# Seven block products in place of eight in a feed-forward up-projection, with ScalarE and VectorE preparing their operands

## The reference

```python
def swiglu(h, w_up, w_down):
    gate, val = jnp.split(h @ w_up, 2, axis=-1)
    return (jax.nn.silu(gate) * val) @ w_down
...
        h = rmsnorm(x, norm_ffn[l]) * (1.0 + sc_ffn) + sh_ffn
        x = x + gt_ffn * swiglu(h, w_ffn_up[l], w_ffn_down[l])
    return rmsnorm(x, norm_final)
```

## Time and profile before

| | us |
|---|---|
| median of 3 runs (lowest, highest) | 2607.14 (2605.65, 2610.41) |
| the profiled execution | 2607.23 |
| its span | 2605.5 |
| TensorE busy (matmuls) | 2543.5, 98% of the span |
| VectorE busy | 1892.0, 73% |
| ScalarE busy | 997.7, 38% |
| GpSimd busy | 504.9, 19% |

### The profile page before, as it was taken

How to read it: one execution, slowest core, us unless ns; L and a number is a source line. 1 busy time by engine, 2 the same in 40 slices (tenths; PEclk the granted TensorE clock), 3 DMA queues, 4 the chain that set the end, 5 groups by cost and what they waited for, 6 DMA issues and landing times.

```text
span 2605.5 us, 44201 instructions
## 1 busy us (share of the span) xinstructions
PE 2543.5 (98%) x16256; PEld 2260.3 (87%) x16256; DVE 1892.0 (73%) x3606; ACT 997.7 (38%) x2220; POOL 504.9 (19%) x440
## 2 busy tenths in 40 slices
PE   6999999999999999999999999999999999999998
PEld 4899889889899989989989989989888888888887
DVE  5688778878878877777777777885666666666666
ACT  6643744654474373364355345333400000000002
POOL 1000401311220130000000000000344444433330
PEclk9999999999999999999999999999999999999999
DMA  7221231132122122223123213241121111111111
GB/s 238 61 65 30 58 80 38 36 94 50 33 70 62 26 57 80 43 50 86 42 48 87 46 33 97 71 135 51 50 65 49 49 45 46 48 49 49 49 41 65
DMA packets 221703, 160.85 MB, mean 62 GB/s; under 512 B 24720, under 2 KB 204024, under 8 KB 221488
## 3 DMA queue, kind: packets, MB, share of 16 engines
q1 hardware_dynamic: 208592, 149.98, 19.8%
q0 software_dynamic: 12896, 8.05, 3.1%
HBM read 141.67 MB, written 16.33 MB: 61 GB/s over the span
## 4 chain that ended last, share of the span: by engine, by line
PE 78%; DVE 14%; ACT 6%; issue 1%; DMA 1%; SPq 0%; DVEq 0%; ACTq 0%
PE bank L180 31%; PE bank L172 21%; PE bank L2191 9%; PE bank L1256 2%; PE bank L1009 2%; PE bank L1262 2%; DVE sig L1089 2%; PE bank L1590 1%; PE bank L1605 1%; PE bank L1213 1%; PE bank L1608 1%; PE bank L1606 1%; DVE feat_region L1702 1%; PE bank L1756 1%; DVE rows_region L1098 1%
## 5 line engine op out<-in xcount | busy, mean ns | idle before, releaser
L172 PE MATMUL bank<-wA_hi,h_hi 128*128 128x256 f32 x1024 | 296.5, 290 | 1.0 <-ACT sig L1061 0.4
L172 PE MATMUL bank<-wB_hi,h_hi 128*128 128x256 f32 x1024 | 296.4, 289 | 0.5 <-ACT sig L1061 0.2
L172 PE MATMUL bank<-wB_lo,h_hi 128*128 128x256 f32 x1024 | 295.5, 289 | 0.0
L172 PE MATMUL bank<-wA_lo,h_hi 128*128 128x256 f32 x1024 | 295.2, 288 | 0.0
L172 PE MATMUL bank<-wB_hi,h_lo 128*128 128x256 f32 x1024 | 295.0, 288 | 0.0
L172 PE MATMUL bank<-wA_hi,h_lo 128*128 128x256 f32 x1024 | 295.0, 288 | 0.0
L180 PE MATMUL bank<-h_hi,wA_hi 128*128 128x512 f32 x672 | 266.0, 396 | 3.1 <-DVE feat_region L1022 1.9
L180 PE MATMUL bank<-h_hi,wB_lo 128*128 128x512 f32 x672 | 265.7, 395 | 0.0
L180 PE MATMUL bank<-h_hi,wA_lo 128*128 128x512 f32 x672 | 265.7, 395 | 0.0
L180 PE MATMUL bank<-h_hi,wB_hi 128*128 128x512 f32 x672 | 265.7, 395 | 0.0
L180 PE MATMUL bank<-h_lo,wA_hi 128*128 128x512 f32 x672 | 265.4, 395 | 0.0
(11 more groups left out here) (394 smaller groups left out, 6042.8 us busy)
## 6 DMA issues: line engine op xcount, KB each, us to landing
w_raw<-in_w_in_dram SPq DMA_DIRECT2D x96, 512.0 KB, 4.0
w_raw<-in_w_ffn_up_dram SPq DMA_DIRECT2D x44, 512.0 KB, 3.9
rows_region<-in_ada_w_dram SPq DMA_DIRECT2D x64, 256.0 KB, 2.8
w_raw<-in_w_ffn_down_dram SPq DMA_DIRECT2D x22, 512.0 KB, 3.5
ada<-in_ada_w_dram SPq DMA_DIRECT2D x8, 1024.0 KB, 14.5
conv_in<-row_scratch SPq DMA_DIRECT2D x16, 512.0 KB, 4.5
rows_region<-in_x_dram SPq DMA_DIRECT2D x8, 512.0 KB, 6.8
w_raw<-in_w_in_dram SPq DMA_DIRECT2D x16, 256.0 KB, 2.9
```

The costliest lines, as they stand in the source:

```text
L172: mm = nc.tensor.matmul(bank[:, n_out:n_out + n1 - n0], (h_hi, h_lo)[hp][:, k, t * P:t * P + P], buf[wp][:, k, n0:n1], start=(s == 0), sto ...
```

## The change

The feed-forward part goes from 11 steps of 256 features to 22 groups of 128. Groups 0 to 3 (`PLAIN`) compute gate and value as before, each unit as two products of 4 blocks. In groups 4 to 21 gate and value, for both halves of the tokens, are treated as one 2 x 2 product of blocks: the weights are x11, x12 (gate columns, lower and upper 512 rows) and x21, x22 (value columns), the activations y11, y12, y21, y22 (lower or upper 512 features, first or second half of the tokens). It is computed with seven block products (12 matmuls each) in place of eight, over sums of weights and of activations (t1 to t4).

- The sums of activations are made once, by VectorE, between its other work of groups 1 to 4 (`make_t1` to `make_t4`, `sum_low`), their high parts by ScalarE (`sum_high`).
- The sums of weights are made in every group by GpSimd (`ffn_pool`), into a ring of four slots of [128, high and low, 4, 128], each of which is refilled when TensorE has read it.
- The high parts of x11 and x12 of each group after the first (`weight_high`), and of the down weight (`down_high`), are made by ScalarE.
- The sigmoid is now three steps of ScalarE (exp, ln(1+.), exp). VectorE no longer adds one and takes a reciprocal.
- Partial results are copied out of the banks by ScalarE (`p1_buf`, `u2_buf`, `p5_buf`, `u3_buf`) and added on VectorE. The down-projection of a group comes after the third product of the next one, with 3 matmuls for each output, and VectorE does 16 additions in every group.
- In the prologue two pieces of `ada_w` share a semaphore, and TensorE waits for both before the first.

```diff
@@ prologue @@
-        sp.dma_start(ada_buf[m][:], ada_v[:, :, o:o + ADA_W]).then_inc(sem(f"ada_in{m}"), 16)
+        sp.dma_start(ada_buf[m][:], ada_v[:, :, o:o + ADA_W]).then_inc(sem(f"ada_in{m // 2}"), 16)
...
-        pe.wait_ge(sem(f"ada_in{m}"), 16)
+        pe.wait_ge(sem(f"ada_in{m // 2}"), 32)
@@ ffn_sp @@
+        for g in range(F_GROUPS):
+            sp.wait_ge(sem("w_split"), slots_made(g))
+            if g + 1 < F_GROUPS:
+                for j in range(2):
+                    load_half(sp, j, up_cols(g + 1)[j])
+            if g == 0:
+                sp.wait_ge(sem("xt_up"), H0 + 2 * KT)
+                sp.dma_start(d_raw, down_v[:, 0]).then_inc(sem("d_in"), 16)
+            sp.wait_ge(sem("w_split"), d_made(g))
+            if g + 1 < F_GROUPS:
+                sp.dma_start(d_raw, down_v[:, g + 1]).then_inc(sem("d_in"), 16)
...
@@ ffn_pool: low_part is one subtraction, parts a cast and a low_part, do waits for the own last one @@
+            if g == 0:
+                pool.wait_ge(sem("w_in0"), 16 * (IN_ALL + 1))
+                parts(0, x11)
+                parts(1, x12)
+            else:
+                pool.wait_ge(sem("taken"), x_high(g, 0))
+                low_part(n, x11)
+                pool.wait_ge(sem("taken"), x_high(g, 1))
+                low_part(n + 1, x12)
+            pool.wait_ge(sem("w_in1"), 16 * (IN_ALL + 1 + g))
+            if plain(g):
+                if g:
+                    down_low(g - 1)
+                slot_free(n + 2)
+                parts(n + 2, x21)
+                slot_free(n + 3)
+                parts(n + 3, x22)
+            else:
+                slot_free(n + 2)
+                do(tt(raw_of(n + 2, 0), x21, x22, ALU.add))
+                do(tt(raw_of(n + 2, 1), raw_of(n + 2, 0), x11, ALU.subtract))
+                do(tt(x12, x12, raw_of(n + 2, 1), ALU.subtract))
+                parts(n + 2, raw_of(n + 2, 1))
+                down_low(g - 1)
+                slot_free(n + 3)
+                do(tt(raw_of(n + 3, 1), x21, x22, ALU.add))
+                parts(n + 3, raw_of(n + 3, 1))
+                do(tt(x21, x11, x21, ALU.subtract))
+                slot_free(n + 4)
+                parts(n + 4, x21)
+                slot_free(n + 5)
+                parts(n + 5, x12)
+                slot_free(n + 6)
+                parts(n + 6, x22)
+            pool.wait_ge(sem("d_in"), 16 * (g + 1))
...
+                pool.wait_ge(sem("down"), 2 * NT * g)
+            do(tt(d_raw, d_raw, gates_ffn, ALU.mult))
@@ ffn_pe: product is 12 matmuls and waits for its slot, down(g) 16 x 3 and waits for hid_lo and down_read @@
+        for g in range(1, PLAIN):
+            pe.wait_ge(sem("gate_taken"), 2 if g == 1 else 2 * g - 1)
+            plain_unit(UP[2], g, 0, 1)
+            pe.wait_ge(sem("hid_full"), 2 * g - 1)
+            plain_unit(UP[3], g, 1, 1)
+            down(g - 1)
+            pe.wait_ge(sem("gate_taken"), 2 * g)
+            plain_unit(UP[1], g, 0, 0)
+            pe.wait_ge(sem("hid_full"), 2 * g)
+            plain_unit(UP[0], g, 1, 0)
+        for g in range(PLAIN, F_GROUPS):
+            a = first_bank(g)
...
+            add(a, 0, "y11", True, False)
...
+            add(UP[1], 1, "y21", True, True)
+            pe.wait_ge(sem("taken"), took(g, P1_COPY))
+            pe.wait_ge(sem("h_lo"), H_DONE + SUM_AT["t2"] + KH)
+            add(a, 2, "t2", False, False)
+            down(g - 1)
+            pe.wait_ge(sem("gate_taken"), 2 * g)
+            pe.wait_ge(sem("h_lo"), H_DONE + SUM_AT["t1"] + KH)
+            add(UP[2], 3, "t1", True, False)
+            pe.wait_ge(sem("taken"), took(g, U2_COPY))
+            add(a, 4, "t3", False, False)
+            pe.wait_ge(sem("taken"), took(g, P5_COPY))
+            add(UP[2], 5, "y22", False, True)
+            pe.wait_ge(sem("taken"), took(g, U3_COPY))
+            add(a, 6, "t4", False, True)
+        down(F_GROUPS - 1)
@@ ffn_act, groups 4 to 21 @@
+            act.wait_ge(sem("up"), up_done(g, 1))
+            act.wait_ge(sem("hid_lo"), 2 * g)
+            step(A(p1_buf[:], a[:], ACT.Copy), "taken")
...
+            act.wait_ge(sem("up"), up_done(g, 3))
+            step(A(u2_buf[:], a[:], ACT.Copy), "taken")
+            act.wait_ge(sem("gate_taken"), 2 * g + 1)
+            sigmoid(p1_buf[:])
+            act.wait_ge(sem("up"), up_done(g, 4))
+            step(A(p5_buf[:], UP[2][:], ACT.Copy), "taken")
+            act.wait_ge(sem("up"), up_done(g, 5))
+            step(A(u3_buf[:], a[:], ACT.Copy), "taken")
+            down_high(g)
+            if g + 1 < F_GROUPS:
+                weight_high(g + 1)
+            act.wait_ge(sem("gate_taken"), 2 * g + 2)
+            sigmoid(u2_buf[:])
+            hid_high(g, 1, 1, u2_buf)
+            hid_high(g, 2, 0, p1_buf)
@@ ffn_dve, one block of a sum, and groups 4 to 21 @@
+        def make_t1(k):
+            step(tt(h_tmp("t1", 0, k), h_in("y12", 0, k), h_in("y11", 0, k), ALU.subtract))
+            step(tt(h_tmp("t1", 1, k), h_in("y12", 1, k), h_in("y11", 1, k), ALU.subtract))
+            step(tt(h_tmp("t1", 1, k), h_tmp("t1", 1, k), h_tmp("t1", 0, k), ALU.add), "h_full")
...
+            if g == PLAIN:
+                make_t1(3)
+                sum_low("t1", 0)
+                sum_low("t1", 1)
+                sum_low("t1", 2)
+            dve.wait_ge(sem("up"), up_done(g, 2))
+            dve.wait_ge(sem("taken"), took(g, P1_COPY))
+            step(tt(p1_buf[:], p1_buf[:], UP[1][:], ALU.add), "gate_taken")
+            for n in range(2 * NT):
+                down_add(g - 1, n)
+                if g == PLAIN and n == 3:
+                    sum_low("t1", 3)
+            dve.wait_ge(sem("gate_exp"), 2 * g + 1)
+            step(tt(p1_buf[:], p1_buf[:], e_one, ALU.mult))
+            dve.wait_ge(sem("taken"), took(g, U3_COPY))
+            step(tt(u3_buf[:], u3_buf[:], p5_buf[:], ALU.add))
+            dve.wait_ge(sem("up"), up_done(g, 6))
+            step(tt(u2_buf[:], u2_buf[:], UP[2][:], ALU.add), "gate_taken")
+            dve.wait_ge(sem("gate_exp"), 2 * g + 2)
+            step(tt(u2_buf[:], u2_buf[:], e_one, ALU.mult))
+            step(tt(u2_buf[:], u2_buf[:], u3_buf[:], ALU.mult), "hid_full")
+            dve.wait_ge(sem("up"), up_done(g, 7))
+            step(tt(p1_buf[:], p1_buf[:], a[:], ALU.mult), "hid_full")
+            hid_low(g, 1, 1, u2_buf)
+            hid_low(g, 2, 0, p1_buf)
+        for n in range(2 * NT):
+            down_add(F_GROUPS - 1, n)
+            if n % 2 and n >= 5:
+                final_norm(n // 2 - 2)
```

More of the change, by code:

```diff
@@ L2084, in _build @@
     UP, DOWN = banks[0:4], banks[4:8]
[L2085 removed]
     IN_ALL = len(groups)
[L2088 to L2095 removed]
+    F_GROUPS = D_FF // P
+    PLAIN, SLOTS, KH = 4, 4, KT // 2
+    slots = [over(f"slot_{n}", [P, 2, KH, P], F32R, at_byte["wA_hi"] + n * 4096) for n in range(SLOTS)]
@@ new lines, in ffn_pool, with product, plain_unit, down @@
+        down_low(F_GROUPS - 1)
+    def ffn_pe(pe):
+        def product(bank, g, n, name, first, last):
+            pe.wait_ge(sem("w_split"), slot_made(g, n))
+            slot = slots[(slot0(g) + n) % SLOTS]
+            for k in range(KH):
+                if g == 0 and name in ("y12", "y22"):
+                    pe.wait_ge(sem("h_lo"), H1 + KT + (0 if name == "y12" else KH) + k + 1)
+                for s, (wp, hp) in enumerate(PASSES):
+                    mm = nc.tensor.matmul(bank[:], slot[:, wp, k], h_block(name, hp, k), start=(first and k == 0 and s == 0),
+                                          stop=(last and k == KH - 1 and s == 2), skip_group_check=True)
+            return mm
+        def plain_unit(bank, g, gv, half):
+            product(bank, g, 2 * gv, ("y11", "y12")[half], True, False)
+            product(bank, g, 2 * gv + 1, ("y21", "y22")[half], False, True).then_inc(sem("up"), 1)
+        def down(g):
+            pe.wait_ge(sem("w_split"), d_made(g))
+            pe.wait_ge(sem("hid_lo"), 2 * g + 2)
@@ L2194, in ffn_pe @@
-                mm.then_inc(sem("down"), 1)
+                if 2 * NT * g + n >= 4:
+                    pe.wait_ge(sem("down_read"), 2 * NT * g + n - 3)
+                for s, (wp, hp) in enumerate(PASSES):
+                    mm = nc.tensor.matmul(DOWN[n % 4][:], hid[hp][:, t * P:t * P + P],
+                                          D_W[wp][:, half * HALF:half * HALF + HALF], start=(s == 0), stop=(s == 2))
+                mm.then_inc(sem("down"), 1)
+        for u in range(2):
+            pe.wait_ge(sem(f"proj_read{u}"), (N_UNITS - u + 1) // 2)
@@ L2200, in ffn_act @@
             nrm_hi(act, step, n)
[L2201 to L2209 removed]
+        act.wait_ge(sem("up"), up_done(0, 1))
```

365 lines of the change are left out of this document (251 added, 114 removed).

## The result

Four runs of the changed kernel gave a median of 2648.40 us (2647.26 to 2650.26), four of the kernel before 2608.19: a ratio of 1.0155, interval 1.0138 to 1.0173. The forecast was 2620, range 2592 to 2634: right in sign, short by 28 us, and outside the range. The profiled execution took 2647.26 us with a span of 2645.5. (Its lines have other numbers: a product is L2283, the down-projection L2299, a low part on GpSimd L2213. "t2" as a step of TensorE is the product over the sum of activations t2, the third of a group and the last one ahead of the down-projection; "t3" is the fifth. A group's period is the time from its t2 to the next group's.)

What follows compares the result with a forecast made beforehand. TensorE bounded the kernel before. The ledger was -49.0 matmuls, +34.0 waits, +7.2 group 4, +11 groups 1 to 3, +4 and +7 end, +0.5 prologue, -0.8 group 0: 2620 us, range 2592 to 2634.

Steps and rivals of the forecast that it cites:

- TensorE's own sum: Feed-forward matmuls: 49.0 us removed; TensorE's own period with seven products 30.24 us.
- GpSimd's chain: Loop from t3 through ScalarE and GpSimd to the next t2: closes at 30.96 us, above TensorE's 30.24 by 0.72.
- The lock of 4 x 0.32: Four VectorE two-input SBUF operations collide with GpSimd's burst, 0.32 us each: 1.28 more, period 32.24, wait 2.0 ahead of t2.
- Second in line, the p1 copy: ScalarE's p1 copy, waiting for hid_lo: ready 6.8 us into a group, wanted at 5.44, still within the wait for t2's slot.
- First seam, last down-projection's wait: TensorE waits 5.7 us for group 1's first slot and 4.0 us for hid ahead of the last down-projection.
- Groups 1 to 4 as a whole: Waits and restarts add 11 us in groups 1 to 3; group 4 takes 7.2 us beyond 30.24.
- Prologue: TensorE waits for pairs of ada_w loads: 0.5 us more, bounds 0 and 1.1.
- The faster rival's times: Lock not met: period 30.96 and 2587 us, or 2575 with GpSimd below 30.24; chance 0.18.
- The end: From the last down-projection's start to the end: 26.9 us, VectorE's additions and scalings the bound.
- Slower still: the clock: Half rate after TensorE's waits: 2624 us for three waits over 3.5 us, 2647 if 2.0-us waits too; chance 0.10.
- The sum of 2618.8: Forecast span in us: 2001.9 to group 4, then 37.4 + 548.1 + 4.0 + 26.9 + 0.5.
- The case of half rate behind every 2.0-us wait: Dearer part of the clock rival: 18 x 1.5 = 27 us lost in the groups with sums, 2647 us.

Runs made afterwards that it cites:

- the kernel with one-column low parts: Changed kernel with VectorE's low parts of the hidden values made for one column only in the groups with sums: 2610.19 us.
- the seven-filler kernel: Changed kernel plus seven unread matmuls ahead of t2 in every group with sums, filling TensorE's wait: 2625.99 us, ratio 1.0068.
- the one with p1 first: Changed kernel with p1's product, low part and high part made first, and the next p1 copy right behind that high part: 2620.55 us.

## Why the forecast was wrong

- **TensorE's own sum**: right, 216 matmuls fewer. The period of 30.24 was 0.22 too long, mostly because the down-projection's 0.2333 us a matmul did not carry over.
- **GpSimd's chain**: right. The wait ahead of t2 on its slot was 1.89 us, forecast 2.0; the period where the clock held 32.20, forecast 32.24.
- **The lock of 4 x 0.32**: right in size, by the kernel with one-column low parts (0.67 for two).
- **Second in line, the p1 copy**: right, and closer than it looked; with ScalarE's order changed or GpSimd relieved it became first at 2.7 and 4.05 us.
- **First seam, last down-projection's wait**: right (5.76 against 5.7, 3.94 against 4.0). The 5.7 is less than its own parts, 1.6 + 2.4 + 0.7 + 1.5 = 6.2 before handovers.
- **Groups 1 to 4 as a whole**: right within 2 us, in part by luck. The waits were some 4 us shorter than forecast, and 5.2 us at half rate, which the sum doesn't have, came in their place. In group 4 the two waits were 2.54 and 1.80 us; the forecast names 2.4 and 4.4, which is 6.8, and adds 7.2.
- **Prologue**: mis-sized. 0.5 was forecast with bounds 0 and 1.1, and the last product with the modulation weights ended 1.9 later in the changed kernel's trace; how much of it the pairs cost stays open.
- **The faster rival's times**: by its own terms, 18 x 1.28 and 5 less than 2620, it comes to 2592 and not 2587. No part of the 2620 rests on it.
- **The end**: 28.8 against 26.9, of which 0.6 is VectorE's later start behind matmuls at 0.58 of the clock; the rest lies in small waits between its additions and in the last transfer (4.2 against 3.95).
- **The step that failed is the rival "Slower still: the clock"**, and the argument by which it got 0.10: "after the idle 1.86 before 1865.52 it stayed 1.00". The sum of 2618.8 has nothing for the clock behind the 17 waits of 2.0 us; measured were 22.4 us, in 14 of the 17. The case of half rate behind every 2.0-us wait was priced almost right (18 x 1.5 = 27 us, 2647 against 2648.4 measured) and given next to no chance. One row was read as if it told what such a wait does, while it was one draw. In the other eleven traces the same first feed-forward product was drawn again. Ten had a wait of 2.58 us ahead of it, and its 24 matmuls took 5.7 us in five of them and 7.0 to 7.3 in the other five. One had the 1.86 of the kernel before, and kept its clock as that one did; so the row itself was no accident as far as two draws tell, but it did not carry over to the waits ahead of t2. Two of the chain's rows, of the seven-filler kernel and of the one with p1 first, with the same wait of 2.58 us ahead of each:

```profile
1867.96 5.72 PE bank L2283 x24
```

```profile
1864.81 7.33 PE bank L2283 x24
```

The Trainium skill's page "TensorE: Matmul & The Clock Gate", section "HAM oscillation — how this bites in real kernels", describes a loop whose matmuls fall back to the half rate after each of its waits. Those waits, for transfers, take about 3 to 5 us by that page, so it spoke for the forecast's three waits over 3.5 us and not for those of 2.0, to which the forecast applied it. The changed kernel does it in 14 of 17 groups, behind waits of 1.9 us; the kernels with waits of 1.2 and 1.56 us do not, so by these runs the pattern sets in at shorter waits than the page's, and holds for some waits of a loop and not for others.

The chance of 0.70 for slower was borne out; the range, which took in the clock for three waits only, ended 14 us too low; the 14 groups with a slow t2 cost 22.

## What to carry to other kernels

Where a change leaves a short periodic wait on TensorE, price it twice, with and without the half rate behind it, and do not let a single row decide which; here the waits were 32 us in all and the clock behind them 22. What such a wait costs beyond itself can be had back without curing its cause, by matmuls in the gap, even useless ones. When several engines feed one product, follow the second chain as well before relieving the first: taking GpSimd's work away, or starting it earlier, cost 56 and 16 us here. Relieving the second chain alone gained 28 us against the changed kernel, relieving both 58, and only the latter beat the kernel before.

## What was not expected of the hardware

- A granted clock that falls behind idle times of 1.88 to 1.90 us in 14 groups and not in 3 whose waits, neighbours and instructions are the same. In the changed kernel the spared ones lie 167.4 us apart both times; with waits of 2.7 us they lie otherwise (2052, 2294 and 2396 us). What decides between them is open; no run was aimed at it.
- The loss in t2 also grew with the wait: at most 1.6 us behind 1.9 us; up to 2.5 behind 2.7, in 2 of 17 groups; over 2 in 12 of 17 behind 4.05.
- 512-column matmuls of the down-projection at 0.2267 us with its bank changed every three, and 0.2333 with a change every six; why is open.
- The same kernel part, the 1860 us ahead of the feed-forward, ends at times that lie 4.3 us apart from one profiled execution to another among the eleven traces with the pairs (first product at 1864.81 to 1869.09).
